# Fourteen projections of a fused two-layer kernel, turned round so that tokens are stationary and 512 weight columns move

## The reference, cut to what matters

```
h = rms_norm(x, norm_g)                     # 256 x 1024
proj = h @ w_in                             # blocks of 512 columns and some narrow ones
y_a, y_b, y_c, y_d = four branches of proj, each 256 x 512
branch_d = einsum('nbsw,nwd->bsnd', ys, w_branch)
g = sigmoid(gates)                          # gates: the last 4 x 1024 columns of proj
merged = sum(g * branch_d, axis=2)
return x + merged @ w_out
```

## Time and profile before

| what | value |
|---|---|
| median of 3 runs | 1201.8 us (1201.57 to 1202.69) |
| profiled execution, span from first to last instruction | 1201.2 us |
| PE busy | 1056.9 us (88%) |
| DVE / ACT / POOL busy | 491.7 / 356.6 / 387.8 us |
| HBM read | 301.89 MB |

### The profile page before, as it was taken

The page is one execution under the profiler, slowest core; times in us unless marked ns, Lnnn a source line. Parts: engine busy times, 40 slices in busy tenths (PEclk is TensorE's granted clock), DMA queues, the critical chain, the costliest instruction groups (busy, mean ns, idle before and its releaser), DMA issues.

```text
span 1201.2 us, 20207 instructions
## 1 busy us (share of the span) xinstructions
PE 1056.9 (88%) x8237; PEld 852.8 (71%) x8237; DVE 491.7 (41%) x973; ACT 356.6 (30%) x536; POOL 387.8 (32%) x176
## 2 busy tenths in 40 slices
PE   9999999999999999999999998977676676767776
PEld 7999999999999999798989787443333333333334
DVE  4447944701125886667854413221111111111113
ACT  4544253444447557234252103100000000000002
POOL 4867568887877766133030000000000000000000
PEclk8999899999999998999999999998888888888898
DMA  6645446466656444113221685999999999999994
GB/s 232 197 127 157 121 143 201 148 185 185 191 167 205 154 143 140 53 54 140 80 91 43 276 332 213 417 428 428 428 428 428 428 428 429 428 428 428 428 413 178
DMA packets 41552, 303.95 MB, mean 253 GB/s; under 512 B 4869, under 2 KB 5253, under 8 KB 27786
## 3 DMA queue, kind: packets, MB, share of 16 engines
q1 hardware_dynamic: 41194, 302.43, 66.4%
q10 hardware_dynamic: 288, 0.52, 0.1%
HBM read 301.89 MB, written 1.05 MB: 252 GB/s over the span
## 4 chain that ended last, share of the span: by engine, by line
PE 60%; DMA 27%; DVE 8%; issue 1%; ACT 1%; SPq 1%; POOL 1%; DVEq 0%; ACTq 0%; POOLq 0%
DMA arena<-down 20%; PE bank L447 11%; PE bank L448 11%; PE bank L449 11%; PE bank L818 9%; PE bank L1273 4%; DMA weights<-gate_up 4%; PE bank L1256 3%; DMA arena<-gate_up 3%; PE bank L782 1%; DVE arena L1948 1%; PE bank L1227 1%; PE bank L1285 1%; PE bank L1018 1%; PE bank L997 1%
## 5 line engine op out<-in xcount | busy, mean ns | idle before, releaser
L2733 POOL TENSOR_TENSOR rounded<-weights,rounded 128x1024 fp32r<-128x1024 f32 x152 | 368.6, 2452 | 175.7 <-ACT rounded L1350 164.0
L447 PE MATMUL bank<-rounded 128*128 128x256 f32 (+2 forms) x784 | 223.0, 284 | 0.7 <-POOL rounded L2733 0.7
L449 PE MATMUL bank<-rounded 128*128 128x256 f32 (+2 forms) x784 | 221.7, 283 | 0.0
L448 PE MATMUL bank<-rounded 128*128 128x256 f32 (+2 forms) x784 | 221.5, 282 | 0.0
L1350 ACT ACTIVATE rounded<-weights 128x1024 fp32r<-128x1024 f32 x146 | 147.1, 1052 | 85.0 <-PE bank L449 56.0
L447 PEld LDWEIGHTS bank<-rounded 128*128 128x128 f32 (+1 forms) x784 | 147.8, 189 | 2.9 <-POOL rounded L2733 1.2
L448 PEld LDWEIGHTS bank<-rounded 128*128 128x128 f32 (+1 forms) x784 | 147.1, 188 | 0.6 <-issue 0.5
L449 PEld LDWEIGHTS bank<-rounded 128*128 128x128 f32 (+1 forms) x784 | 146.7, 187 | 0.2
L447 PE MATMUL bank<-rounded,rounded 128*128 128x256 f32 (+3 forms) x456 | 131.8, 289 | 2.1 <-DVEq L2178 0.8
L448 PE MATMUL bank<-rounded,rounded 128*128 128x256 f32 (+3 forms) x456 | 130.4, 286 | 0.0
L449 PE MATMUL bank<-rounded,rounded 128*128 128x256 f32 (+3 forms) x456 | 130.2, 286 | 0.0
(11 more groups left out here) (444 smaller groups left out, 1348.5 us busy)
## 6 DMA issues: line engine op xcount, KB each, us to landing
weights<-front SPq DMA_DIRECT2D x152, 512.0 KB, 4.3
arena<-down SPq DMA_DIRECT2D x30, 2048.0 KB, 20.6
weights<-gate_up SPq DMA_DIRECT2D x28, 2048.0 KB, 33.4
arena<-gate_up SPq DMA_DIRECT2D x28, 2048.0 KB, 33.2
weights<-front SPq DMA_DIRECT2D x8, 2048.0 KB, 8.3
arena<-gate_up SPq DMA_DIRECT2D x4, 1536.0 KB, 32.9
weights<-gate_up SPq DMA_DIRECT2D x4, 1024.0 KB, 15.3
arena<-down SPq DMA_DIRECT2D x4, 1024.0 KB, 8.0
```

The lines of the kernel that those rows point to most:

```text
L447: nc.tensor.matmul(out, a[0], b[1], start=start, stop=False)
L448: nc.tensor.matmul(out, a[0], b[0], start=False, stop=False)
L449: return nc.tensor.matmul(out, a[1], b[0], start=False, stop=stop)
L2733: nc.gpsimd.tensor_tensor(lo, raw[q % RAW], hi.bitcast(f32), ALU.subtract).then_inc(sem("w_lo"), 1)
```

## The change

Fourteen blocks (`dv`, `av`, eight gate blocks, four branch blocks) are multiplied with 128 tokens stationary and 512 weight columns moving. `dv`, `av` and the gates are laid out by rows, so a half now holds 4 of the 8 k-tiles with all 512 columns; a matmul fills a whole bank. A new `branch_tok` does the same for the branches. For the gates both fills of a block now read both halves; the buffer of half 0 is released by a new semaphore `half_read`, but carries the order of the second fill. `merged` is now laid out with tokens on partitions, and 16 transposes on PE (`turn_merged`, in two groups of 8) turn it back into the layout of the output product; ACT and DVE round and split it from the transposed banks. `wo0` and `wo1` are interleaved: half of `wo0`, second group of transposes, half of `wo1`, rest of both.

```diff
+class Use:
+    def __init__(self, name, count, order):
+        self.name, self.count, self.order = name, count, order
...
             def project_tok(names, b):
-                fs = [begin(name, PJ, 2 * b + i) for i, name in enumerate(names)]
-                readers[2 * b] = fs[1]
+                fs = [begin(name, PJ, 2 * b + 1) for name in names]
+                readers[2 * b] = Use("half_read", half_reads.pop(0), fs[1].order)
                 for half in range(2):
                     w = halved(b, half)
                     for t, f in enumerate(fs):
-                        for k in range(KD):
-                            last = matmul3(f.bank[:, half * SEQ:(half + 1) * SEQ], [m[:, k, t * P:(t + 1) * P] for m in h1],
-                                           [m[:, k * SEQ:(k + 1) * SEQ] for m in w], k == 0, k == KD - 1)
+                        for kk in range(KD // 2):
+                            k = half * (KD // 2) + kk
+                            last = matmul3(f.bank[:, :], [m[:, k, t * P:(t + 1) * P] for m in h1],
+                                           [m[:, kk * W1:(kk + 1) * W1] for m in w], k == 0, k == KD - 1)
                         if half == 1:
                             end(f, last)
+                    if half == 0:
+                        last.then_inc(sem("half_read"), 1)
+
+            def branch_tok(names, b, ys):
+                for half in range(2):
+                    w = halved(b, half)
+                    for t in range(TT):
+                        f = begin(names[2 * half + t], PJ, 2 * b + half)
+                        for k in range(CW):
+                            last = matmul3(f.bank[:, :], [m[:, k, t * P:(t + 1) * P] for m in ys],
+                                           [m[:, k * W1:(k + 1) * W1] for m in w], k == 0, k == CW - 1)
+                        end(f, last)
...
+            def turn_merged(half):
+                pe.wait_ge(sem("merged"), 4 * 3 + 2 * half + 2)
+                for i in range(2):
+                    f = begin(f"mT{2 * half + i}", ((3,), (4,), (7,))[(2 * half + i) % 3])
+                    for j in range(2):
+                        for t in range(TT):
+                            c = (2 * half + t) * W1 + (2 * i + j) * P
+                            last = nc.tensor.transpose(f.bank[:, j * SEQ + t * P:j * SEQ + (t + 1) * P], merged_cols[:, c:c + P], ident)
+                    end(f, last)
+
             for n in ORDER:
                 for half in range(2):
-                    project_T([f"g{n}{2 * half + j}" for j in range(2)], GATE[n] + half, h1, SEQ)
+                    project_tok([f"g{n}{2 * half + j}" for j in range(2)], GATE[n] + half)
                 pe.wait_ge(sem(f"y{n}"), 2)
-                project_T([f"br{n}{j}" for j in range(4)], WB[n], (y_hi[n], y_lo[n]), SEQ, stride=D, kk=CW)
...
+                branch_tok([f"br{n}{j}" for j in range(4)], WB[n], (y_hi[n], y_lo[n]))
+                if n == ORDER[3]:
+                    turn_merged(0)
+            w, f = halved(WO, 0), begin("wo0", PJ, 2 * WO)
+            pe.wait_ge(sem("merged"), 4 * 4 + 2)
             for j in range(2):
-                last = part_products(f, w, 0, h1_all, (KD - 2, KD - 1), j, 2, SEQ)
+                part_products(f, w, 0, h1, range(KD // 2), j, 2, SEQ)
+            turn_merged(1)
+            f.order = len(fills)
+            w_next, f_next = halved(WO, 1), begin("wo1", PJ, 2 * WO + 1)
+            for j in range(2):
+                part_products(f_next, w_next, 0, h1, range(KD // 2), j, 2, SEQ)
+            pe.wait_ge(sem("merged"), 4 * 4 + 4)
+            for j in range(2):
+                last = part_products(f, w, 0, h1, range(KD // 2, KD), j, 2, SEQ)
             end(f, last)
-            project_T(["wo1"], WO, h1_all, SEQ, column=2 * P)
-            project_T(["wo2", "wo3"], WO + 1, h1_all, SEQ)
+            for j in range(2):
+                last = part_products(f_next, w_next, 0, h1, range(KD // 2, KD), j, 2, SEQ)
+            end(f_next, last)
+            project_T(["wo2", "wo3"], WO + 1, h1, SEQ)
...
+            def merged_low(j):
+                f = got(f"mT{j}")
+                dve.wait_ge(sem("h_hi"), 4 + j + 1)
+                js = slice(2 * j, 2 * j + 2)
+                link(nc.vector.tensor_tensor(h1_lo_r[:, js], two(f.bank), h1_hi_r[:, js].bitcast(f32), ALU.subtract))
+                dve.sem_inc(free[f.b], 1)
+                dve.sem_inc(sem("merged"), 1)
```

More of the change, by code:

```diff
@@ L142, in build @@
         fills, uses, turn, readers = {}, [0] * 8, {}, {}
+        half_reads = list(range(1, 11))
         def fill(name, pool, block=None):
@@ L225, in build @@
         psum = {a: stat(TT * NH) for a in "fb"}
-        merged, merged_lo_r = chunked(both(KD * SEQ), KD)
+        merged_cols = g_(KD * SEQ)
+        merged = merged_cols.rearrange("p (k t) -> p k t", k=KD)
         top[0] = layer_base
@@ L674, in _ @@
[L674 to L678, removed]
-            for j in range(2):
-                last = part_products(f, w, 0, h1_all, (KD - 2, KD - 1), j, 2, SEQ)
+                branch_tok([f"br{n}{j}" for j in range(4)], WB[n], (y_hi[n], y_lo[n]))
@@ L845, in meta_level @@
                 if v == 0:
-                    pe.wait_ge(sem("m_am"), 1)
+                    pe.wait_ge(sem("m_rows"), 2)
                 else:
@@ L1346, in lead @@
                         before = readers[h - SPLIT]
-                        act.wait_ge(full[before.b], before.n + 1)
+                        if isinstance(before, Use):
+                            act.wait_ge(sem(before.name), before.count)
+                        else:
+                            act.wait_ge(full[before.b], before.n + 1)
                     for q in (2 * h, 2 * h + 1):
@@ L1481, in _ @@
             for j in range(4):
-                lead_for(f"br{ORDER[3]}{j}")
-                act.wait_ge(sem("merged"), 4 * 3 + 2 * j + 1)
-                nc.scalar.activation(h1_hi_r[:, 2 * j:2 * j + 2, :], two(fills[f"br{ORDER[3]}{j}"].bank),
-                                     ACT.Copy).then_inc(sem("h_hi"), 1)
+                f = got(f"mT{j}")
+                nc.scalar.activation(h1_hi_r[:, 2 * j:2 * j + 2, :], two(f.bank), ACT.Copy).then_inc(sem("h_hi"), 1)
             for j in range(4):
@@ L2081, in _ @@
                     link(nc.vector.tensor_tensor(two(f.bank), two(f.bank), g, ALU.mult))
-                    if i < 3:
-                        link(nc.vector.tensor_tensor(m, two(f.bank), m, ALU.add))
-                        dve.sem_inc(free[f.b], 1)
-                        dve.sem_inc(sem("merged"), 1)
-                        continue
-                    link(nc.vector.tensor_tensor(two(f.bank), two(f.bank), m, ALU.add))
-                    dve.sem_inc(sem("merged"), 1)
-                    dve.wait_ge(sem("h_hi"), 4 + j + 1)
-                    js = slice(2 * j, 2 * j + 2)
-                    link(nc.vector.tensor_tensor(merged_lo_r[:, js], two(f.bank), h1_hi_r[:, js].bitcast(f32), ALU.subtract))
+                    link(nc.vector.tensor_tensor(m, two(f.bank), m, ALU.add))
                     dve.sem_inc(free[f.b], 1)
                     dve.sem_inc(sem("merged"), 1)
+            def merged_low(j):
+                f = got(f"mT{j}")
+                dve.wait_ge(sem("h_hi"), 4 + j + 1)
[3 more added lines that the diff above has]
+                dve.sem_inc(sem("merged"), 1)
+            for j in range(4): merged_low(j)
             for j in range(4):
@@ L2291, in meta_a @@
                 link(last)
-                dve.sem_inc(sem("m_am"), 1)
+                dve.sem_inc(sem("m_rows"), 1)
             def meta_t(v):
@@ L2948, in lay_out @@
     front = [in_halves(np.concatenate([w["bc"], w["wi"], w["df"], w["ki"], pad, w["qi"]], 1))]
-    front += [in_halves(w[n]) for n in "bq dq dk dv av au az dz bz cb cc cx cz".split()]
+    front += [(by_rows if n in ("dv", "av") else in_halves)(w[n]) for n in "bq dq dk dv av au az dz bz cb cc cx cz".split()]
     for n in (0, 3, 2, 1):
-        front += parts(w["gates"][:, n * D:(n + 1) * D]) + [in_halves(I["w_branch"][0, n])]
+        front += whole(w["gates"][:, n * D:(n + 1) * D]) + [in_halves(I["w_branch"][0, n])]
     front += parts(I["w_out"][0])
```

7 lines of the change are left out of this document (2 added, 5 removed).

## The result

The changed kernel takes 1225.57 us (median of 4 runs, 1224.89 to 1227.31) against 1201.68 us (4 runs of the kernel before on the same chip, 1199.1 to 1202.69): a ratio of 1.0202, 95% interval 1.0184 to 1.0221. The profiled execution of the change has a span of 1225.1 us, 23.9 longer than the earlier trace rows.

A forecast was written before the change was run, and what follows sets the result against it. PE was taken to set the pace of the gate and branch stage and the output product. Terms -2.2 + 1.4 + 20.6 + 1.7 = +21.5 us on 1201.8 gave 1223.3 us, range 1209 to 1235.

The forecast's parts named there:

- one to one: Before 600 us: a microsecond won or lost moves the kernel's end by about a microsecond.
- Part 1: Matmuls in the fourteen blocks: one of 512 columns takes 216 ns, against 119.7 for 256; a half block 5.2 us.
- `dv` and `av`: The two blocks ahead of the gates: faster matmuls gain 2 x 1.1 us, DVE's chain moves along; term -2.2 us.
- Part 2: Gate and branch stage: late splits make a 7.0 us weight chain, PE stands 1.8 us eight times; +1.4 us.
- Part 3: End of the merge: transposes +3.5 us, PE's stand before `wo0` +5.6, clock fall behind it +2.2.
- Part 4: Before `wo3`: half 55 is split late, PE stands for POOL +7.1 us, clock fall behind it +2.2.
- Clock: One fall among eight gate-stage stands, +1.7 us; one behind each long stand at the end, +2.2 each.
- (a): Gate stage: the weight chain does not bind, the change is faster, 1192.7 us; chance 0.09 including mixtures that win.
- (b): Matmul: the wide one gains nothing at 240 ns, +10.2 us per the gate stage, 1234 us; chance 0.07.
- (c): End: only half comes true, half 55 or 54 in time or no clock fall; 1214 or 1217.2 us; chance 0.17.
- (d): Gate stage: the clock falls at most of the eight stands, 1230 to 1235 us; chance 0.14 together with 226 ns.
- (e): Whole kernel: the times balance within the measurement, needing an end that costs 1 us only; chance 0.03.

The follow-up runs named there:

- the probe: Changed kernel plus six series of 24 unused matmuls of rounded operands, 128 to 512 moving columns, 128 or 32 stationary, at one gate block's end; 1251.91 us.
- `dvav_release`: Kernel before the change, still 256 columns, with only the early release of half 0's buffer for `dv` and `av`; 1198.59 us, ratio 0.997.
- `gate_early`: Changed kernel, with ACT making one of the two splits ahead of both evacuations in the gate blocks; 1214.52 us, ratio 1.0104.
- `end_54`: Changed kernel, with ACT's split of half 54 moved behind the copies of the turned `merged`; 1225.2 us, ratio 1.0204.
- `end_55`: Changed kernel, with half 55 (weights of `wo3`) split behind the work on `wo0`, ahead of that on `wo1`; 1222.25 us, ratio 1.018.
- `all_fixed`: Changed kernel with the edits of `gate_early` and `end_55`, half 54 split behind the copies, first eight transposes and low parts ahead of the last branch fill's merge; 1199.62 us.
- `end_both`: Changed kernel with the moves of `end_54` and `end_55` together; 1217.28 us, ratio 1.0149.
- `early_end`: Changed kernel with the edits of `gate_early`, `end_54` and `end_55` together; 1204.48 us, ratio 1.0014.

## Why the prediction was right and wrong

Direction, range and size came true: 1223.3 forecast, 1225.57 measured. The size owes something to luck: the gate stage came out 5.7 us worse than booked, the end 2.1, the part ahead of the stage 0.6 and the rest 0.7 us better.

**What bounds it, and one to one.** Right: 822.75 and 822.07 us behind `wo3`.

**Part 1, width.** Wrong. "I take 216, because that row has the same 512 cycles" failed: the probe shows 234.5 ns. The 119.7 ns for the narrow one was slightly low as well, since a window counts the matmuls in flight at its edges: from start to start it is 120.2. The row chosen was plain fp32, and the loss of the earlier trace rows, which I called per matmul, is mostly per column. The two widths of the trace, 256 and 272, lie too close to tell the two kinds of loss apart (16 columns make 6.7 ns at 0.417 a column and 7.2 at 0.45), so the rows allowed 216 and 240 alike, and the choice went by a row of another operand type. Twelve blocks won 3.3 us once nothing else bound, not 13.4. Of these 10 us about 7 reach the stage by the prediction's own formula (4 x 36.5 us against 4 x 34.8), because the first half of two blocks in three lies under the weight chain.

**`dv` and `av`.** The term was -2.2, the trace has -2.8, by another way. "It moves along" and "would be hidden anyway" both failed: the width gives about 0.25 us a block, and `dvav_release` shows that the early release does the rest, by removing the two stands.

**Part 2, the weight chain.** The mechanism is confirmed by `gate_early`, which removes it with one line. The places (second half of G1 and of B) and the releaser were right, the chain's length too. The stands were 1.4 instead of 1.8 us because PE's half took 5.63 instead of 5.2 us. The sum, +1.4 for the stage (with the clock +3.1), was +8.8: 48 matmuls at 234.5 ns make a block 0.9 us longer than I had it, and where the chain does not bind, this counts. Put 234.5 into the prediction's own formula: 11.26 + 2 x (7.0 + 5.63) = 36.5 a branch, four times 146.1; the first matmul behind each of eight stands took 0.1 us more, and the stage 147.2.

**Part 3.** The stand before `wo0` was 6.26 where I had 5.6, ended by DVE as forecast. The transposes were over-sized: "8 transposes of two records at 110 ns" are eight records in all, 0.9 us a group, 1.8 in place of 3.5. The sentence in the part on precision that transposes leave two records each is wrong: the row counts eight for eight transposes. The sum of both, 7.1 us from the last branch matmul to `wo0`, matches the 7.4. `end_54` shows a second limit that I had not seen behind the first: DVE's own order leaves 3.06 us.

**Part 4.** Right: 6.63 against 7.1 us, ended by POOL; `end_55` leaves 1.28.

**Clock.** Two falls at the end, as forecast: 3.5 and 4.4 us of work at 213 ns a matmul in place of 120 lose about 1.5 and 1.9 us, against 2.2 each. None in the gate stage (PEclk 1.00 there), where 1.7 had been put in. For the whole end 20.6 us were forecast and 18.5 measured; the transposes make 1.7 of the difference and the clock 1.0, the stands 0.2 the other way.

**Rivals.** (a), faster, needed both a chain of 5.2 us and a matmul of 216; the probe rules out the second and the earlier trace rows the first. (b) was nearly right about the matmul: its stage of 4 x 37.0 = 148 us compares with 147.2. Its total of 1234 held besides a fall of the clock in that stage (1.7), the transposes counted twice (1.7) and no gain at `dv` and `av` (2.8); without these it gives 1227.8. (c) and (d) did not come: both waits and both falls are there, and none of the eight. Where the wide form is given nearly all it needs (`all_fixed`), the result is near (e), 2.95 us below the kernel before, and no gain over `dvav_release`.

## What to carry to other kernels

When an edit changes which fill releases a buffer, walk the next in-order queue (here ACT) and write down what is now queued ahead of the work that the pacing engine waits for: here an order that put two evacuations ahead of a split cost 12 us in the gate stage. Price a wider instruction by rows of the same operand type at two widths far apart; where the trace has none, keep the bound of no gain as likely as the other. And when a stand is repaired, look for the next engine behind it before booking the whole of it.

## What the runs showed of the hardware

- Rounded fp32 operands: 111.7, 118.7, 176.7 and 234.5 ns for 128, 256, 384 and 512 moving columns at the level of 2.4 GHz; from 256 to 128 columns the time hardly falls. At the granted clock of 0.50 sixteen matmuls of 256 columns take 3.4 us, 213 ns each: 256 cycles of 1.2 GHz, with no loss left.
- The clock fell behind one stand of 3.06 us (`end_54`) and not behind two others of the same length (`end_both`, `early_end`).
- Transposes of 128x128 fp32 start every 0.11 us at a granted clock of 1.00 and leave one record each.
- DVE beside POOL. The kernel before, timelines of POOL and DVE:

```profile
102.06 29.62 POOL L2733 TENSOR_TENSOR rounded<-weights,rounded 128x1024 fp32r<-128x1024 f32 x11 [6.44 <-ACT rounded L1350]
...
119.11 2.77 DVE L2011 TENSOR_TENSOR arena<-arena 128x512 f32<-128x512 f32 x1
121.80 7.67 DVE L1948 SCALAR_TENSOR_TENSOR arena<-arena 128x256 f32<-128x256 f32 x3
```

and `dvav_release`, the same operations:

```profile
112.05 4.99 POOL L2746 TENSOR_TENSOR rounded<-weights,rounded 128x1024 fp32r<-128x1024 f32 x2 [0.17 <-ACT rounded L1363]
119.97 4.89 POOL L2746 TENSOR_TENSOR rounded<-weights,rounded 128x1024 fp32r<-128x1024 f32 x2 [2.93 <-ACT rounded L1363]
...
117.62 0.69 DVE L2024 TENSOR_TENSOR arena<-arena 128x512 f32<-128x512 f32 x1
118.23 2.04 DVE L1961 SCALAR_TENSOR_TENSOR arena<-arena 128x256 f32<-128x256 f32 x4
```

With POOL at work without a pause the addition took 2.77 us and three of the following operations 7.67; in POOL's pause from 117.04 to 119.97 they took 0.69, and four of them 2.04. In `dvav_release` itself the same line took 2.78 us at 109.66, where POOL was at work. The early release, which opens the pause, so shortens DVE's chain, and the stand at 153 is gone. The Trainium skill (SBUF — State Buffer, "SBUF: two separate sides") says that DVE and GpSimd share a pair of ports that one holds for a whole instruction; the 2.1 us that the addition lost fit into one POOL instruction of some 2.4 us. That the port is the cause is argued from these rows; no run took POOL's work away alone.
